# DIFF layers: the sub-norm's weights move from GpSimd's multiply into the copies of the turned blocks, and the first mixed block is turned one step sooner

## The chip, the cores and the metric
One core of one Trainium2 chip. The metric is the device time in microseconds (us) of one execution of the whole program. Every time in the profile is counted from the start of the span. PE is TensorE, DVE is VectorE, ACT is ScalarE, POOL is GpSimd, and SP is SyncE, which issues all the loads.

## The reference
Six transformer blocks run one after the other over 256 tokens of width 1024, all in float32. Blocks 0 and 1 have a hybrid mixer (HYB), block 1 with a mixture of eight experts. Blocks 2 to 5 are the second model's: differential attention (DIFF), MoBA, sliding window with sinks (SWA), and DIFF again, each followed by an MLP. What is changed lies in DIFF:

```python
p = jax.nn.softmax(s, axis=-1)
p = p[:, :, 0] - lam * p[:, :, 1]          # two maps of a head, combined
o = einsum('bhqk,bkhe->bqhe', p, v)        # 8 heads of width 128
o = rms_norm(o, sub_g) * (1.0 - lambda_init)
return o.reshape(B, S, H * DIFF_V_DIM) @ w_out
```

`sub_g` has 128 values, one per channel of a head, the same for all 8 heads. `rms_norm` divides each head's 128 channels of a token by their root mean square and multiplies by `sub_g`.

## The kernel before
Every product is made of three: both operands are split into a high part (ACT copies into the reduced type, `xt_hi`, `whi`) and a low part (DVE subtracts, `xt_lo`, `wlo`), and PE multiplies high by high, low by high and high by low. Weights come in units of 128 x 2048 (`load`), each split by ACT (L1691, L1695) and DVE (L2116, L2122) ahead of its use. Each engine's program is written out by hand; the engines meet only through semaphores, and within an engine everything stays in the written order.

In a DIFF layer (l = 2 and l = 5, n = 16 maps, two to a head) `soft_heads` of each engine runs over steps i. For a pair of maps j, j+1 (j even):

- PE turns the heads (`turn_heads`, L1468, at even i), makes the scores (`pair_scores`, L1593 and L1595, step j+1), turns the combined map (`turn_pair`, L1568, step j+5) and multiplies by the values (`pair_values`, L1580 to L1582, step j+6).
- DVE masks the scores and takes their maximum (L2551, step j+1), combines the two maps of a head (`combine`, L2471, step j+3), and in `finish_pair` (L2482 to L2491, step j+5) divides by the sum, takes the sum of squares of a head, asks for the ratio of the pair j+4 (`ask_ratio`, L2500, which waits for that pair's exponentials) and asks for the root.
- ACT copies the turned heads (L1806), takes the exponentials (L1821, L1823, map j at step j+2), and copies the turned map (L1839, step j+5).
- POOL runs `diff_norms`: per head the ratio of the pair two heads ahead (L711, L712), the root (L692), the block of y times the root (L729), and that block times `subg` (L730); then it raises `normed`.

The output projection needs y turned, in four mixed blocks of 128 x 512 (`turn_mixed`): PE transposes (L798) after enough heads are `normed` (4, 4, 6, 8 for blocks 0 to 3), ACT copies the high part (L1711), DVE takes the low part (L2140). Block 0 holds heads 0 to 3 of token tile 0, block 1 the same heads of tile 1, blocks 2 and 3 hold heads 4, 5 and 6, 7 of both tiles. `out_rows(l, n, t, parts)` multiplies unit n of `w_out` by the turned blocks of token tile t (L921); a part is one half of the unit, six matmuls of 512 columns. Block 0 is turned at step 15 = n-1, block 1 at step 18 = n+2; the two halves of `out_rows(l, 0, 0)` stand at steps 17 and 19. `out_project_diff` (L977) follows: rows of unit 1, block 2, half a unit for tile 1, block 3, and the rest.

`subg` is loaded once by broadcast to all partitions (L594), and the setup on DVE multiplies it by 1 - lambda_init (L2425). SP's loads of layer weights stand behind it in SP's queue.

Of the kernel before, what the change touches and what calls it, by code (L numbers as in the profile page):

```python
# [14 lines left out]
P = 128  # L15
# [157 lines left out]
def build(nc, A, out, bias_scratch):  # L173
    with ExitStack() as ctx:  # L174
        def sb(name, shape, dt=F32, scope=ctx):
            return scope.enter_context(nc.sbuf_tensor(name, shape, dt))
# [15 lines left out]
        sinks = sb("sinks", [P, 16])  # L192
        minus_sinks = sb("minus_sinks", [P, 16])
        lam = sb("lam", [P, 16])
        subg = sb("subg", [P, 2, 2 * HD])
        pos_i = sb("pos_i", [P, NT], I32)
        rope_f = sb("rope_f", [P, 6, NT, 8])
        rope_k = sb("rope_k", [P, NT, 8], I32)
# [222 lines left out]
        def mixed_cols(x_t, l, s):  # L421
            if s < 2 and KIND[l] != HYB:
                return x_t[:, 0:4, s * P:(s + 1) * P]
            n = mixed_block(l, s)
            return x_t[:, 2 * n:2 * n + 2, :].rearrange("p k (t s) -> p t k s", t=NT)
# [112 lines left out]
        def _(sp):  # L538
# [50 lines left out]
            def small():  # L589
                sp.dma_start(pos_i[:], A["positions_2"][0].rearrange("(t p) -> p t", p=P),  # L590
                             allow_slow_non_contiguous=True).then_inc(got["pos"], 16)
                for i, n in enumerate(("diff_lam_q1_2", "diff_lam_k1_2", "diff_lam_q2_2", "diff_lam_k2_2")):
                    sp.dma_start(lam_in[:, i], A[n].partition_broadcast(P)).then_inc(got["lam"], 16)
                sp.dma_start(subg[:], A["diff_subln_g_2"].partition_broadcast(P)).then_inc(got["subg"], 16)  # L594
                sp.dma_start(router_w[:], A["moe_router"][0].rearrange("(k p) e -> p k e", p=P)).then_inc(
                    got["router"], 16)
                sp.dma_start(sinks[:], A["swa_sinks_2"][0].partition_broadcast(P)).then_inc(got["sinks"], 16)
# [84 lines left out]
        @block.gpsimd  # L682
        def _(pool):
            pool.wait_ge(cst_loaded, 16)
            done = [0]

            def roots(n):
                for _ in range(n):
                    r = done[0]
                    w = ROOTS[r]  # L690
                    pool.wait_ge(var_ready, r + 1)
                    pool.tensor_tensor(rstd[:, r % 8, 0:w], var[:, r % 8, 0:w], cst[:, C_HALF:C_HALF + w],  # L692
                                       ALU.pow).then_inc(root_ready, 1)
                    done[0] += 1

            def stick_masks(l):
                for p in range(NSTICK[KIND[l]] // 2):
                    pool.wait_ge(z_read, HEAD0[l] + 2 * p + 2)
                    if p < 2:

                        pool.wait_ge(qk_turned, HEAD0[l] // 2 + 3)
                    else:
                        pool.wait_ge(pool_out, l + 1)
                    pool.tensor_tensor(stick_a(p), stick_z(p), stick_mask(C_STRICTNEG), ALU.add).then_inc(zm_ready, 1)

            def ratio(l, h):

                d = DIFF_SLOT[l]
                pool.wait_ge(var_ready, done[0] + 1)
                second = rinv[:, :, 2 * h + 1:2 * h + 2]  # L710
                link(pool.tensor_tensor(second, second, sums[:, :, 2 * h:2 * h + 1], ALU.mult))  # L711
                pool.tensor_tensor(second, second, lam[:, 10 + d:11 + d].rearrange("p c -> p c ()").broadcast_to([P, NT, 1]),  # L712
                                   ALU.mult).then_inc(root_ready, 1)
                done[0] += 1

            def diff_norms(l):

                ratio(l, 0)
                ratio(l, 1)
                for h in range(8):  # L720
                    if h + 2 < 8:
                        ratio(l, h + 2)
                    r = done[0]
                    roots(1)
                    pool.wait_ge(root_ready, r + 1)
                    v = y[:, :, h * P:(h + 1) * P]
                    scale = rstd[:, r % 8, 0:NT].rearrange("p t -> p t ()").broadcast_to([P, NT, P])
                    gains = subg[:, DIFF_SLOT[l]].rearrange("p c -> p () c").broadcast_to([P, NT, P])
                    link(pool.tensor_tensor(v, v, scale, ALU.mult))  # L729
                    ins = pool.tensor_tensor(v, v, gains, ALU.mult)  # L730
                    ins.then_inc(normed, 1)

            chain = [0]

            def link(ins):

                chain[0] += 1
                ins.then_inc(pchain, 1)
                pool.wait_ge(pchain, chain[0])

            for l in range(NL):
                if KIND[l] != HYB:
                    roots(2)
                if KIND[l] == SWA:
                    pool.wait_ge(rope_sin, 1)
                    pool.wait_ge(proj_ev, EV0[l + 1])
                    rotate(pool, link, [(8, 8)], late_tmp).then_inc(late_rope_done, 1)
                stick_masks(l)
                if KIND[l] == DIFF:
                    diff_norms(l)  # L750
                if l == 1:
                    roots(2)
                    pool.wait_ge(t_lo, 4 * 5)
                    for t in range(NT):
                        for half in range(2):
                            pool.memset(y[:, t, half * 512:(half + 1) * 512], 0.0).then_inc(added, 1)
                    roots(4)
                else:
                    roots(6 if KIND[l] == HYB else 2)
            roots(2)  # L760
# [3 lines left out]
        def _(pe):  # L764
# [21 lines left out]
            def turn_mixed(l, s):  # L786


                if KIND[l] in (MOBA, SWA):
                    pe.wait_ge(o_read, OG0[l] + (2, 2, 3, 4)[s])  # L790
                else:
                    pe.wait_ge(normed, NORMED0[l] + ((4, 4, 6, 6) if KIND[l] == HYB else (4, 4, 6, 8))[s])
                for i in range(4):
                    if s < 2 and KIND[l] != HYB:
                        t, k = s, i
                    else:
                        t, k = i // 2, 2 * mixed_block(l, s) + i % 2
                    mm = pe.transpose(bank[turned_at(l)[s]][:, i * P:(i + 1) * P], y[:, t, k * P:(k + 1) * P], ident)  # L798
                mm.then_inc(turned, 1)
# [672 lines left out]
            def soft_heads(l):  # L1472
# [3 lines left out]
                for i in range(n + (5 if kind == DIFF else 4)):  # L1476
# [38 lines left out]
                    if kind == DIFF:  # L1515
                        if i % 2 == 1 and 0 <= i - 5 < n:
                            turn_pair(l, i - 5)
                        if i == n - 2:
                            pe.wait_ge(proj_ev, EV0[l + 1])
                        if i % 2 == 0 and 0 <= i - 6 < n:  # L1520
                            pair_values(l, i - 6)
                        if i in (n - 1, n + 2):
                            turn_mixed(l, (i - n + 1) // 3)
                        if i == n + 1:
                            pe.wait_ge(t_lo, 4 * (3 * l + 1) + 1)
                            out_rows(l, 0, 0, (0,))
                        if i == n + 3:
                            out_rows(l, 0, 0, (1,))
                    j = i - 3
                    if 0 <= j < n and kind != DIFF:  # L1530
# [143 lines left out]
        def _(act):  # L1674
# [33 lines left out]

            def turn_mixed(l, s):
                act.wait_ge(turned, 4 * (3 * l + 1) + s + 1)  # L1710
                act.activation(mixed_cols(xt_hi, l, s), mixed_bank(l, s), ACT.Copy).then_inc(t_hi, 1)  # L1711

            def high_of_tokens(t):
                act.activation(xn_hi[:, t], x[:, t], ACT.Copy).then_inc(xn_hi_ready, 1)
# [93 lines left out]
            def soft_heads(l):  # L1808
                kind = KIND[l]
                n = NSOFT[kind]  # L1810
                for i in range(max(n + (4 if kind == DIFF else 3), late_parts(l) + 6)):
# [24 lines left out]
                    if 0 <= j < n and kind == DIFF and j % 2 == 0:  # L1836
                        s = SOFT0[l] + j
                        act.wait_ge(pt_done, s + 2)
                        act.activation(pt[:, s % 4], pt_bank(l, j)[:, 0:384], ACT.Copy).then_inc(pt_ready, 2)  # L1839
                    if kind == DIFF and i in (n - 1, n + 2):  # L1840
                        turn_mixed(l, (i - n + 1) // 3)
                    for u, half in late_used(l, i):
                        if kind == HYB or u != PLAN.proj[l][-1][-1]:
                            hi(u + NH, (half,))
# [254 lines left out]
        def _(dve):  # L2099
# [4 lines left out]
            def link(ins):  # L2104

                chain[0] += 1
                ins.then_inc(dchain, 1)
                dve.wait_ge(dchain, chain[0])
# [28 lines left out]

            def turn_mixed(l, s):
                dve.wait_ge(t_hi, 4 * (3 * l + 1) + s + 1)
                dve.tensor_tensor(mixed_cols(xt_lo, l, s), mixed_bank(l, s), mixed_cols(xt_hi, l, s).bitcast(F32),  # L2140
                                  ALU.subtract).then_inc(t_lo, 1)

            def ask_root(src, scale, eps, w):

# [245 lines left out]
            def setup():  # L2390
# [31 lines left out]
                    link(dve.tensor_scalar(lam[:, 10 + d:11 + d], lam[:, 8 + d:9 + d], -LAMBDA_INIT[l], None, ALU.add))  # L2422
                dve.wait_ge(got["subg"], 16)
                for l, d in DIFF_SLOT.items():
                    link(dve.tensor_scalar(subg[:, d], subg[:, d], 1.0 - LAMBDA_INIT[l], None, ALU.mult))  # L2425

            def add_bias(l, c, t):

# [100 lines left out]
            def soft_heads(l):  # L2529
# [8 lines left out]
                for i in range(n + 4):  # L2538
# [36 lines left out]
                    if i == n + 2 and kind == HYB:  # L2575
                        for s in range(2):
                            turn_mixed(l, s)
                    if i == n - 1 and kind == DIFF:
                        turn_mixed(l, 0)
                    j = i - 4  # L2580
                    if 0 <= j < n and kind != DIFF:
# [422 lines left out]
```

## Time and profile before

| | us |
|---|---|
| median of 3 runs | 2429.32 |
| lowest, highest | 2429.15, 2430.7 |
| the profiled execution | 2427.38 |
| its span, first to last instruction | 2425.6 |
| PE busy in the span | 2393.6 |
| DVE, ACT, POOL busy | 1725.7, 1450.1, 94.3 |

The span is the time between the first and the last instruction; the rest of an execution's time lies around it. Busy time of PE is modelled from pipelined matmuls, so a busy PE is not PE at its peak. A row of the timeline gives the start, the duration, the engine, the line, the operation, output and inputs, how many were merged, and in brackets the idle time before with who ended it. Starts of neighbouring rows are the better measure of pace, since ends of pipelined instructions overlap the next ones.

### The profile page before, as it was taken

The page shows a single profiled execution, that of the slowest core. Times are in us where ns is not written, and L with a number is a line of the kernel's source. Part 1 is how long each engine was busy: PE and PEld are TensorE (multiplying, and loading weights), DVE is VectorE, ACT ScalarE, POOL GpSimd, SP SyncE. Part 2 cuts the span into 40 slices and gives each one's busy share as a digit, 9 for nine tenths or more (in the row PEclk, how much of TensorE's full clock was granted, in tenths as well). Part 3 has the DMA queues.
Part 4 walks back from the last instruction along what each step waited for, and adds up shares of the span by engine and source line. Part 5 has one row for each costly group of instructions (what it writes and reads, how often), then busy time and mean ns, then how long its engine had stood idle before and what let it go on. Part 6 is the DMA issues. An engine that isn't in the chain of part 4 may idle for free. (4 is left out here: it accounts for less than half of the span.)

```text
span 2425.6 us, 31990 instructions
## 1 busy us (share of the span) xinstructions
PE 2393.6 (99%) x12546; PEld 2017.5 (83%) x12546; DVE 1725.7 (71%) x1911; ACT 1450.1 (60%) x1662; POOL 94.3 (4%) x130
## 2 busy tenths in 40 slices
PE   9999999999999999999999999999999999999998
PEld 7889978888888888888877788888888788887887
DVE  5565456888898998988995865666656665568565
ACT  6454354588888888888865554454444554456442
POOL 1000010000000000000000300000000000004000
PEclk9999999999999999999999999999999999999999
DMA  9266552699999999999965365452655265553553
GB/s 323 69 204 206 181 208 72 223 348 361 348 350 359 335 360 352 348 350 347 363 244 193 105 217 191 156 200 95 223 191 187 72 211 191 172 205 119 186 191 104
DMA packets 242366, 555.40 MB, mean 229 GB/s; under 512 B 10841, under 2 KB 36849, under 8 KB 241905
## 3 DMA queue, kind: packets, MB, share of 16 engines
q1 hardware_dynamic: 242160, 552.41, 65.5%
q8 instruction: 159, 2.61, 0.4%
q14 instruction: 47, 0.38, 0.0%
HBM read 551.31 MB, written 1.07 MB: 228 GB/s over the span
## 5 line engine op out<-in xcount | busy, mean ns | idle before, releaser
L2116 DVE TENSOR_TENSOR wlo<-raw,whi 128x2048 fp32r<-128x2048 f32 x486 | 1112.8, 2297 | 444.8 <-ACT whi L1691 444.0
L1691 ACT ACTIVATE whi<-raw 128x2048 fp32r<-128x2048 f32 x487 | 933.7, 1925 | 551.2 <-PE bank L921 141.6
L843 PE MATMUL bank<-whi,xt 128*128 128x512 f32 (+1 forms) x1056 | 311.3, 379 | 3.3 <-DVE xt L2133 1.3
L843 PEld LDWEIGHTS bank<-whi,xt 128*128 128x128 f32 x1056 | 189.5, 188 | 40.6 <-issue 3.1
L1234 PE MATMUL bank<-whi,xt 128*128 128x512 f32 (+1 forms) x768 | 222.0, 373 | 0.8 <-DVE e_hf L2744 0.8
L1077 PE MATMUL bank<-xt,whi 128*128 128x512 f32 x768 | 209.1, 394 | 0.0
L843 PE MATMUL bank<-wlo,xt 128*128 128x512 f32 (+1 forms) x528 | 197.6, 374 | 0.0
L921 PE MATMUL bank<-whi,h_hi 128*128 128x512 f32 x596 | 184.8, 391 | 0.0
L921 PE MATMUL bank<-whi,h_lo 128*128 128x512 f32 x596 | 183.9, 390 | 0.0
L921 PE MATMUL bank<-wlo,h_hi 128*128 128x512 f32 x596 | 183.9, 390 | 0.0
L1234 PEld LDWEIGHTS bank<-whi,xt 128*128 128x128 f32 x768 | 138.2, 189 | 24.8 <-DVE e_hf L2744 1.2
L1077 PEld LDWEIGHTS bank<-xt,whi 128*128 128x128 f32 x768 | 133.0, 189 | 19.1
L1234 PE MATMUL bank<-whi,odd_hi 128*128 128x512 f32 (+1 forms) x384 | 144.0, 375 | 0.1
L1234 PE MATMUL bank<-wlo,odd_hi 128*128 128x512 f32 (+1 forms) x384 | 142.9, 372 | 0.0
L1234 PE MATMUL bank<-wlo,xt 128*128 128x512 f32 (+1 forms) x384 | 142.8, 372 | 0.0
L1234 PE MATMUL bank<-whi,odd_lo 128*128 128x512 f32 (+1 forms) x384 | 142.7, 372 | 0.0
L921 PEld LDWEIGHTS bank<-whi,h_lo 128*128 128x128 f32 x596 | 111.9, 188 | 23.9
L921 PEld LDWEIGHTS bank<-wlo,h_hi 128*128 128x128 f32 x596 | 111.9, 188 | 23.7
L1081 PEld LDWEIGHTS bank<-xt,wlo 128*128 128x128 f32 x768 | 117.8, 189 | 16.2
L921 PEld LDWEIGHTS bank<-whi,h_hi 128*128 128x128 f32 x596 | 109.3, 188 | 20.6
L1081 PE MATMUL bank<-xt,wlo 128*128 128x256 f32 x768 | 122.1, 281 | 0.0
L692 POOL TENSOR_TENSOR rstd<-var,cst 128x1 f32<-128x1 f32 (+2 forms) x46 | 37.2, 808 | 2065.8 <-DVE var L2150 2051.1
(345 smaller groups left out, 3834.4 us busy)
## 6 DMA issues: line engine op xcount, KB each, us to landing
raw<-in_moe_wg SPq DMA_DIRECT2D x88, 1024.0 KB, 6.1
raw<-in_moe_wu SPq DMA_DIRECT2D x88, 1024.0 KB, 5.8
raw<-in_moe_wd SPq DMA_DIRECT2D x88, 1024.0 KB, 5.9
raw<-in_mlp_w_up SPq DMA_DIRECT2D x64, 1024.0 KB, 5.3
raw<-in_mlp_w_down SPq DMA_DIRECT2D x64, 1024.0 KB, 4.9
raw<-in_diff_w_in SPq DMA_DIRECT2D x24, 1024.0 KB, 5.2
raw<-in_w_in SPq DMA_DIRECT2D x19, 1024.0 KB, 7.8
raw<-in_moba_w_in SPq DMA_DIRECT2D x12, 1024.0 KB, 5.1
```

Source lines behind the costliest of these rows:

```text
L692: pool.tensor_tensor(rstd[:, r % 8, 0:w], var[:, r % 8, 0:w], cst[:, C_HALF:C_HALF + w], ALU.pow).then_inc(root_ready, 1)
L843: mm = pe.matmul(proj_bank(l, c, t)[:, 0:width], a[:, kx, t * P:(t + 1) * P], b[:, k, :], start=(kx == 0 and i == 0), stop=(kx == KT - 1 a ...
L921: mm = pe.matmul(bank[4 + 2 * t + half][:, :], a[:, k, t * P:(t + 1) * P], b[:, kk, half * 512:(half + 1) * 512], start=begin and i == 0, ...
L1077: pe.matmul(bank[f][:, :], hi[:, k, f * P:(f + 1) * P], xt[:, :, kx, :], start=kx == 0, stop=False, skip_group_check=True)
L1081: mm = pe.matmul(bank[f][:, 0:S], lo[:, k, f * P:(f + 1) * P], xt_hi[:, kx, :], start=False, stop=kx == KT - 1, skip_group_check=True)
L1234: mm = pe.matmul(bank[b][:, 0:width], a[:, kx, t * P:(t + 1) * P], w[:, k, :], start=(kx == 0 and i == 0), stop=(kx == KT - 1 and i == 2))
L1691: act.activation(whi[u % NH][:, :], raw[u % NR][:, :], ACT.Copy).then_inc(hi_ready[u % NR], 2)
L2116: dve.tensor_tensor(wlo[u % NR][:, :], raw[u % NR][:, :], whi[u % NH][:, :].bitcast(F32), ALU.subtract).then_inc(lo_ready[u % NR], 2)
```

## The change
POOL's second multiply per head is gone. `subg` is laid out the other way: channel d of a head stands in partition d, one column per DIFF layer, and since a turned mixed block has a head's channels on its partitions, the gain is a factor per partition there. ACT's copy takes it as its scale (with the function Identity instead of Copy), and DVE's low part becomes turned times gain minus high, in one instruction for blocks 0 and 1 and in two (one for each token tile) for blocks 2 and 3. The other layers keep their copies. Besides, block 0 is turned at step n-2 instead of n-1 on all three engines, and the two halves of the first output rows stand at steps n-1 and n+1 instead of n+1 and n+3.

```diff
-        subg = sb("subg", [P, 2, 2 * HD])
+        subg = sb("subg", [P, 32])
-                sp.dma_start(subg[:], A["diff_subln_g_2"].partition_broadcast(P)).then_inc(got["subg"], 16)
+                sp.dma_start(subg[:, 0:2], A["diff_subln_g_2"].rearrange("d p -> p d"),
+                             allow_slow_non_contiguous=True).then_inc(got["subg"], 16)
@@ POOL, diff_norms
-                    gains = subg[:, DIFF_SLOT[l]].rearrange("p c -> p () c").broadcast_to([P, NT, P])
-                    link(pool.tensor_tensor(v, v, scale, ALU.mult))
-                    ins = pool.tensor_tensor(v, v, gains, ALU.mult)
-                    ins.then_inc(normed, 1)
+                    pool.tensor_tensor(v, v, scale, ALU.mult).then_inc(normed, 1)
@@ PE, soft_heads
-                        if i in (n - 1, n + 2):
-                            turn_mixed(l, (i - n + 1) // 3)
-                        if i == n + 1:
+                        if i in (n - 2, n + 2):
+                            turn_mixed(l, (i - n + 2) // 4)
+                        if i == n - 1:
                             pe.wait_ge(t_lo, 4 * (3 * l + 1) + 1)
                             out_rows(l, 0, 0, (0,))
-                        if i == n + 3:
+                        if i == n + 1:
                             out_rows(l, 0, 0, (1,))
@@ ACT, turn_mixed and soft_heads
-                act.activation(mixed_cols(xt_hi, l, s), mixed_bank(l, s), ACT.Copy).then_inc(t_hi, 1)
+                gain = subg[:, DIFF_SLOT[l]:DIFF_SLOT[l] + 1] if KIND[l] == DIFF else 1.0
+                act.activation(mixed_cols(xt_hi, l, s), mixed_bank(l, s), ACT.Identity if KIND[l] == DIFF else ACT.Copy,
+                               scale=gain).then_inc(t_hi, 1)
-                    if kind == DIFF and i in (n - 1, n + 2):
-                        turn_mixed(l, (i - n + 1) // 3)
+                    if kind == DIFF and i in (n - 2, n + 2):
+                        turn_mixed(l, (i - n + 2) // 4)
@@ DVE, turn_mixed, setup and soft_heads
-                dve.tensor_tensor(mixed_cols(xt_lo, l, s), mixed_bank(l, s), mixed_cols(xt_hi, l, s).bitcast(F32),
-                                  ALU.subtract).then_inc(t_lo, 1)
+                if KIND[l] == DIFF:
+                    gain = subg[:, DIFF_SLOT[l]:DIFF_SLOT[l] + 1]
+                    parts = [(mixed_cols(xt_lo, l, s), mixed_bank(l, s), mixed_cols(xt_hi, l, s))]
+                    if s > 1:
+                        parts = [tuple(a[:, t] for a in parts[0]) for t in range(NT)]
+                    for low, src, high in parts:
+                        ins = dve.scalar_tensor_tensor(out=low, in0=src, scalar=gain, in1=high.bitcast(F32),
+                                                       op0=ALU.mult, op1=ALU.subtract)
+                    ins.then_inc(t_lo, 1)
-                    link(dve.tensor_scalar(subg[:, d], subg[:, d], 1.0 - LAMBDA_INIT[l], None, ALU.mult))
+                    link(dve.tensor_scalar(subg[:, d:d + 1], subg[:, d:d + 1], 1.0 - LAMBDA_INIT[l], None, ALU.mult))
-                    if i == n - 1 and kind == DIFF:
+                    if i == n - 2 and kind == DIFF:
                         turn_mixed(l, 0)
```

## Rows read from the trace of the kernel before

**Rows 1.** The page, part 1: busy time, share of the span, instructions.
```profile
PE 2393.6 (99%) x12546; PEld 2017.5 (83%) x12546; DVE 1725.7 (71%) x1911; ACT 1450.1 (60%) x1662; POOL 94.3 (4%) x130
```

**Rows 2.** PE's waits, whole span: us in total, times, longest us.
```profile
PE bank L1568 <- DVE z L2471: 3.0, 4, 1.2
...
PE bank L921 <- DVE wlo L2122: 0.5, 2, 0.2
```

**Rows 3.** Windows: stretch, length, busy us per engine, clock, DMA share, GB/s.
```profile
2193.00:2227.00 34.00, 31.37 (x190) 24.73 (x189) 29.17 (x104) 21.44 (x60) 20.76 (x34) 1.00 0.19 63
```

**Rows 4.** Timeline, layer 5, DVE and POOL: combinations with and without POOL beside them.
```profile
2193.41 1.74 DVE L2471 SCALAR_TENSOR_TENSOR z<-z,rinv 128x128 f32<-128x128 f32 x2
2193.44 0.61 POOL L729 TENSOR_TENSOR y<-y,rstd 128x256 f32<-128x256 f32 x1
2194.14 0.73 POOL L730 TENSOR_TENSOR y<-y,subg 128x256 f32<-128x256 f32 x1
...
2214.40 0.75 DVE L2471 SCALAR_TENSOR_TENSOR z<-z,rinv 128x128 f32<-128x128 f32 x2 [0.53 <-POOL rinv L712]
```

**Rows 5.** Timeline of PE, layer 5: scores and the next turned pair, twice.
```profile
2194.31 0.60 PE L1595 MATMUL bank<-qk 64*128 64x256 f32 x4
2195.20 0.55 PE L1568 MATMUL bank<-cst,z 128*128 128x128 f32 x3 [0.28 <-DVE z L2471]
...
2199.84 0.60 PE L1595 MATMUL bank<-qk 64*128 64x256 f32 x4
2200.37 0.55 PE L1568 MATMUL bank<-cst,z 128*128 128x128 f32 x3
```

**Rows 6.** Timeline of PE, end of layer 5, from the last heads' turn.
```profile
2205.96 0.60 PE L1468 MATMUL bank<-cst,h_qkv 128*128 128x128 f32 x4
...
2207.92 0.49 PE L1593 MATMUL bank<-qk 64*128 64x128 f32 x4 [0.20 <-DVE nmx L2551]
...
2212.18 0.55 PE L1568 MATMUL bank<-cst,z 128*128 128x128 f32 x3 [1.22 <-DVE z L2471]
2212.78 1.20 PE L921 MATMUL bank<-whi,xt 128*128 128x512 f32 x4
...
2214.27 0.38 PE L1580 MATMUL bank<-h_qkv,pt 128*128 128x128 f32 x2
...
2217.66 1.18 PE L921 MATMUL bank<-whi,xt 128*128 128x512 f32 x4
...
2222.89 0.66 PE L798 MATMUL bank<-cst,y 128*128 128x128 f32 x4 [0.37 <-POOL y L730]
```

**Rows 7.** Timeline of POOL, end of layer 5: the fourth head's multiply.
```profile
2207.89 0.62 POOL L729 TENSOR_TENSOR y<-y,rstd 128x256 f32<-128x256 f32 x1
```

**Rows 8.** Timeline of ACT, end of layer 5: exponential of map 13, first and last.
```profile
2208.14 0.38 ACT L1821 ACTIVATE z<-z,nmx 128x128 f32<-128x128 f32 x1
...
2208.93 0.19 ACT L1823 ACTIVATION_READ_ACCUMULATOR z<-z,nmx 128x1 f32 x1
```

**Rows 9.** Timeline of DVE, end of layer 5: ratio asked, block 0's low half.
```profile
2209.77 0.18 DVE L2500 RECIPROCAL rinv<-sums 128x4 f32<-128x4 f32 x1
...
2212.05 0.68 DVE L2140 TENSOR_TENSOR xt<-bank,xt 128x512 fp32r<-128x512 f32 x1
```

**Rows 10.** ACT's groups by line and shape: busy us, mean ns, idle before.
```profile
L1823 ACT ACTIVATE z<-z,nmx 128x256 f32<-128x256 f32 x76 | 37.7, 496 | 0.0
...
L1737 ACT ACTIVATE h_mix<-bank 128x256 f32<-128x256 f32 x8 | 3.0, 380 | 5.7 <-PE bank L843 5.7
```

**Rows 11.** DMA issues: size and median us from issue to landing.
```profile
subg<-in_diff_subln_g SPq DMA_DIRECT2D x1, 128.0 KB, 6.3
...
pos_i<-in_positions SPq DMA_DIRECT2D x1, 1.0 KB, 4.6
```

**Rows 12.** ACT by line: duration ns min/median/max, first and last start us.
```profile
L1821 ACT ACT_TABLE_LOAD  x1: 1283/1283/1283, 1317.4 to 1317.4; - x1
...
L1862 ACT ACTIVATE h_f<-bank x8: 598/602/609, 1390.9 to 2257.6; 128x512 f32<-128x512 f32 x8
```

More of the change, by code:

```diff
@@ L2139, in turn_mixed @@
                 dve.wait_ge(t_hi, 4 * (3 * l + 1) + s + 1)
-                dve.tensor_tensor(mixed_cols(xt_lo, l, s), mixed_bank(l, s), mixed_cols(xt_hi, l, s).bitcast(F32),
-                                  ALU.subtract).then_inc(t_lo, 1)
+                if KIND[l] == DIFF:
[7 more added lines that the diff above has]
+                    ins.then_inc(t_lo, 1)
+                else:
+                    dve.tensor_tensor(mixed_cols(xt_lo, l, s), mixed_bank(l, s),
+                                      mixed_cols(xt_hi, l, s).bitcast(F32), ALU.subtract).then_inc(t_lo, 1)
             def ask_root(src, scale, eps, w):
```

## The prediction

> **What bounds the kernel now.** I read the page's part 1 first: TensorE (PE) is busy for 2393.6 of 2425.6 us [rows 1], so only about 32 us of the span can be won by taking waits away, and whatever delays PE by a microsecond delays the end by one. The second view is the waits of PE over the whole span: the largest single entry is the turned pairs of probabilities (L1568) that wait for VectorE's (DVE's) combination of two maps (L2471), 3.0 us in 4 waits; the low half of a weight (L2122) costs 0.5 in 2 [rows 2]. Both belong to the ends of the two DIFF layers, l = 2 and l = 5, which is all that the diff touches after the setup. The window of the second of these ends, layer 5, shows PE busy 31.37 of 34 us at the full granted clock (1.00, the 2.4 GHz level), DVE 29.17, ACT 21.44 and POOL 20.76 [rows 3]. Layer 2's end is the same to the instruction, 859 us earlier; I work out layer 5 and count it twice. PE's idle time in the window is 34 - 31.37 = 2.6 us, so **5.3 us in both is the most that this change could win**.
>
> In what follows I cut 2200 off: 7.92 is 2207.92.
>
> **The gains multiply leaves POOL.** L730 goes: one of 0.73 us for each of 8 heads in a layer [rows 4], which gives a head's normed block 0.7 us sooner. POOL is not the bound, so what counts is who waits for it. First, DVE. A combination is two instructions that read two tiles each from SBUF. Alone the two take 0.75 us; where POOL's L729 and L730 run beside them they take 1.74 [rows 4]. The start times in that group show how: the first begins with L729 (0.61) and the second is held by L730. Without L730 one of the two stalls stays, 0.6 of L729, and the pair costs about 0.7 + 0.4 = 1.1 instead of 1.74: **0.6 us of DVE back** at each of the three early collisions of a layer. The page "SBUF — State Buffer" of the Trainium skill, section "Who interferes with whom", says that a DVE instruction with two SBUF inputs and a GpSimd instruction that reads SBUF exclude each other for a whole instruction, whichever starts first. By that rule the pair gets back the stall under L730 and no more, 0.6 and not the whole 1.0 by which it is slowed; the two start times in the rows agree.
>
> What PE gets of it before the end: the turned pair at 2195.20 starts 0.89 after L1595, where the next one starts 0.53 after it [rows 5], so 0.36 us of waiting for the combination goes and PE arrives at the last heads' turn (5.96 [rows 6]) 0.36 sooner, at 5.60. DVE gains 0.2 at first (it then waits for ACT's exponentials) and 0.75 by the third collision.
>
> **The end of the layer, step by step.** PE's order after the change is: turn of heads 14 and 15, values 8, *mixed block 0*, scores 14, turned pair 10, *output rows half 0*, values 10, turned pair 12, *output rows half 1*, values 12, mixed block 1, turned pair 14, values 14. No matmul is added or taken away; the question is only where PE stands.
> - Mixed block 0 needs the fourth head's norm. POOL's multiply for it starts at 7.89 now [rows 7] and ends 0.62 later; with DVE's 0.75 it ends at 7.75. PE, which starts scores 14 at 7.92 now behind a wait of 0.20 and a filling of its pipe [rows 6], is free at about 7.2, **waits 0.6** and turns the block at 7.80. Scores 14 then start at 7.80 + 0.4 = 8.20 instead of 7.92, and turned pair 10 at 9.05.
> - On ACT the copy of the block now stands ahead of the exponential of head 13. That one starts at 8.14 now and is done at 9.12 with its two halves and read-outs [rows 8]; behind the copy (8.5 to 9.15) it starts at 9.1 and is done at 10.1, **1.0 later**.
> - Who waits for that: DVE's finish of pair 8 asks for the ratio of heads 12 and 13, which needs that exponential. It asks at 9.77 now [rows 9] and will at 10.15. Only then comes the low half of block 0, 10.3 to 10.95; it starts at 12.05 now.
> - Output rows half 0 wait for that low half: 11.05. PE has nothing from 9.3 to 11.05: **a new wait of 1.7 us**, in the place of the one of 1.2 at 12.18, which goes. A half costs 14.27 - 12.78 = 1.49 [rows 6].
> - So values 10 at 12.5, turned pair 12 at 13.2 (its combination is done by 13.0: scores from 10.9, 1.1 of masks, 1.0 of combination), half 1 at 13.45, values 12 at 14.9, mixed block 1 at 15.6, turned pair 14 at 16.0. Between it and values 14 there is now no output row that covers the copy of the transposed probabilities (ACT has block 1 ahead of it): values 14 at 17.35, **1.1 us of wait**. Output rows of the second unit follow at 17.95; they start at 17.66 now [rows 6]. So this loop costs 0.65 against the 0.36 brought along: 0.3 late.
> - The last head: its sum of squares no longer meets L730 (now 0.5 lost) and POOL's own multiply is gone (0.7). Block 3 is turned at 22.89 now, behind a wait of 0.37 for POOL and a filling of PE's pipe [rows 6]; without it PE would be there near 22.35, so at 22.6 or 22.65 after the change, and the norm is there at about 22.0. **Block 3 at 22.6: 0.3 sooner.** Of this 0.1 is lost in the rows of the last unit, which wait for a weight's low half (0.2 per layer [rows 2]) that ACT starts after its copy of block 3.
>
> Sum: 0.2 us sooner per layer, **0.4 us in both**.
>
> **The copies that change.** ACT's copy of a turned block takes a factor per partition. No row has that form from PSUM; bounds: a plain copy of 128x256 takes 380 ns and an exponential of the same size with a column of biases 496 [rows 10], so between 0 and 0.12 more per copy. I take 0.1 as the exponential also reads a column; it is in the times above. The low half becomes a product and a difference in one DVE instruction. From below it is no dearer than now: it still reads one tile from PSUM and one from SBUF. Blocks 2 and 3 are two instructions instead of one: one start-up more, under 0.1 us, covered by the 2.9 us of output rows of unit 2 that PE has after block 3. The page "ScalarE: Activation LUTs", section "What ACT_TABLE_LOAD costs", puts such a pointer operand at about 93 ns; by it the sum would not change by 0.05.
>
> **The load of the gains** becomes 256 single elements instead of rows. The load of now lands after 6.3 us; the one vector that already comes element by element, the positions, after 4.6 [rows 11]. It is first read in the setup behind layer 0's first dense groups, after the whole of layer 0's output projection, so even ten times the landing is hidden. POOL's and SP's queues wait for nothing new. The scaling in the setup is two columns instead of two rows, 0.1 us of DVE less beside a weight that ACT has not copied yet: nothing.
>
> **Base.** The profiled execution took 2427.38 us outside for a span of 2425.6, and is 1.94 under the median 2429.32 of the runs; the difference of 0.4 is taken off the median: **2428.9 us**.
>
> **Rivals.**
> 1. *The loop bites harder* (to 2430.3, not beyond 2431.5). If DVE's 0.6 does not come back (POOL's remaining multiply falls so that it holds both instructions of a combination, which is free to happen since both engines shift), the fourth norm ends at 8.51, PE turns block 0 at 8.57, and everything behind is 0.8 later than above: 0.5 late per layer at block 3, +1.0. For it: POOL starts within 0.03 us of the combination in the collision shown [rows 4], by the semaphore that both follow, so their order is not chance and stays. Chance 0.17.
> 2. *The gain is larger* (2425.3 to 2427.8). If ACT or DVE reach the new order with less queueing than I have, the 1.7 and the 1.1 us waits shrink; half of each away is 1.4 per layer, 2.8 in both: 2426.1. Against it: the exponential of head 13 is plainly behind the copy in ACT's program. Chance 0.16. The idle time bounds it at 2424.0.
> 3. *A table load on ACT* (slower, about 2437). The copies of the DIFF layers change their function from Copy to Identity, which this kernel never used. The exponentials' set is loaded once at 1317.4 for 1283 ns [rows 12]. If Identity is not in that set, block 0 pays a load before it and one after it (exponentials 13 to 15 follow), and block 1 one more, all on the loop that PE waits for: 3 x 1.28 = 3.85 per layer, 7.7 in both. The point from which it decides: one load at block 0 alone, twice 2.56, is already beyond 0.2%. Against it: Relu (L1862) runs at 1390.9 with the exponentials' set and no load [rows 12]. Chance 0.03. By the same page's section on table sets the cheap functions, identity by name, stand in every set; then this rival is out.
>
> **Chances.** The forecast with a spread of about 0.8 either way has 0.62; the rivals 0.17, 0.16 and 0.03; 0.02 is for what I don't see. A measurement of this kernel can tell about 0.2%, 4.9 us, from no change. Faster by more would need nearly all the idle time: 0.02. Slower by more: the table load, 0.04. Within: 0.94. The range leaves out the table load and the far ends of rivals 1 and 2: 2426.8 to 2431.0; the runs of before alone spread over 1.5 us.
>
> **What would show it.** Right: combinations of about 1.1 us where 1.7 stood; a wait of about 0.6 of block 0's transposes (L798) for POOL's L729; the largest wait of the end, near 1.7, before the first output rows (L921) for DVE's low half; one near 1.1 before the last values (L1580); none before block 3; the stretch from the turn of the last heads to block 3 about 17.0 us as now (16.93). Wrong: ACT_TABLE_LOAD in these windows; combinations still at 1.7; the wait before the first output rows under 1 us.

## The result, and the profile after

| | before | after |
|---|---|---|
| median (us) | 2429.24 of 4 runs | 2448.00 of 4 runs |
| lowest, highest | 2427.96, 2430.70 | 2447.74, 2449.79 |
| span of the profiled execution | 2425.6 | 2448.0 |

After takes 1.008 times as long as before, with a 95% interval of 1.0067 to 1.0093: 18.8 us slower. The forecast was 2428.9, its range ended at 2431.0, and slower by over 0.2% had a chance of 0.04. The prediction was wrong.

The page of after, part 1, against [rows 1]:

```profile
PE 2414.0 (99%) x12546; PEld 2019.9 (83%) x12546; DVE 1721.3 (70%) x1915; ACT 1451.0 (59%) x1662; POOL 82.2 (3%) x114
```

PE has as many instructions as before (12546) and is busy for 20.4 us more. It is idle for 34.0 us, against 32.0. So the loss is no wait: TensorE's own work has grown longer. It did not grow in the windows that the prediction looked at, either. A stretch of 100 us in the middle of the experts, in a layer that the diff does not touch (windows: stretch, length, busy us per engine with instructions, clock, DMA share, GB/s), first before and then after:

```profile
600.00:700.00 100.00, 99.68 (x491) 84.08 (x490) 89.33 (x61) 84.05 (x81) 0.00 (x0) 1.00 0.99 350
```

```profile
600.00:700.00 100.00, 99.70 (x486) 83.21 (x485) 88.20 (x60) 83.31 (x78) 0.00 (x0) 1.00 0.98 346
```

PE is as busy and its clock is the same, but it gets 486 matmuls done instead of 491. PE's groups by line and shape (busy us, mean ns of one, idle before) show which matmuls these are. Before:

```profile
L843 PE MATMUL bank<-whi,xt 128*128 128x512 f32 x896 | 281.4, 395 | 2.5 <-DVE xt L2133 1.3 <-DVE wlo L2116 1.0 <-DVE wlo L2918 0.2
...
L921 PE MATMUL bank<-whi,h_hi 128*128 128x512 f32 x596 | 184.8, 391 | 0.0
L1234 PE MATMUL bank<-whi,odd_hi 128*128 128x512 f32 x320 | 125.8, 393 | 0.0
...
L1312 PE MATMUL bank<-whi,e_hi 128*128 128x512 f32 x352 | 109.4, 390 | 0.1
```

After (two lines up in the file):

```profile
L841 PE MATMUL bank<-whi,xt 128*128 128x512 f32 x896 | 281.3, 395 | 2.5 <-DVE wlo L2116 1.1 <-DVE xt L2133 1.1 <-DVE wlo L2928 0.3
...
L919 PE MATMUL bank<-whi,h_hi 128*128 128x512 f32 x596 | 187.7, 396 | 0.0
L1232 PE MATMUL bank<-whi,odd_hi 128*128 128x512 f32 x320 | 127.4, 398 | 0.0
...
L1310 PE MATMUL bank<-whi,e_hi 128*128 128x512 f32 x352 | 111.1, 395 | 0.1
```

In all of these the weight (`whi`) is the moving operand of 512 columns, and the second name is the stationary one, which PEld loads ahead of the matmul. With `xt` as the stationary operand a matmul of L841 costs what it did (the `xt` matmuls of L1232 are 2 ns dearer in this one execution, 394 for 392, but 392 again in e2_before_shifted below, which is just as slow). With `h_hi`, `e_hi` or `odd_hi` each one costs 5 ns more, and so do their siblings with the low halves. There are 3 x 596 + 3 x 352 + 3 x 320 = 3804 of them, and 3804 x 5 ns = **19.0 us**, which is the loss within 0.2 us.

### The profile page after: what moved, and what is told of

Same layout as the page of the kernel before. It is cut to its first block and busy times, and to the rows that moved or that the text cites. A ratio compares the mean times of both kernels' runs of the same rounds, so it can differ in the third digit from the quotient of the medians.

```text
span 2448.0 us, 31978 instructions
## 1 busy us (share of the span) xinstructions
PE 2414.0 (99%) x12546; PEld 2019.9 (83%) x12546; DVE 1721.3 (70%) x1915; ACT 1451.0 (59%) x1662; POOL 82.2 (3%) x114
## 5 line engine op out<-in xcount | busy, mean ns | idle before, releaser
L841 PE MATMUL bank<-whi,xt 128*128 128x512 f32 (+1 forms) x1056 | 311.2, 379 | 3.3 <-DVE wlo L2116 1.1
L1232 PE MATMUL bank<-whi,xt 128*128 128x512 f32 (+1 forms) x768 | 223.4, 375 | 0.8 <-DVE e_hf L2754 0.8
L841 PEld LDWEIGHTS bank<-whi,xt 128*128 128x128 f32 x1056 | 189.5, 188 | 40.4 <-issue 2.9
L841 PE MATMUL bank<-wlo,xt 128*128 128x512 f32 (+1 forms) x528 | 197.5, 374 | 0.0
L1232 PEld LDWEIGHTS bank<-whi,xt 128*128 128x128 f32 x768 | 138.8, 189 | 25.3 <-DVE e_hf L2754 1.2
L1232 PE MATMUL bank<-whi,odd_hi 128*128 128x512 f32 (+1 forms) x384 | 145.5, 379 | 0.1
L1232 PE MATMUL bank<-wlo,odd_hi 128*128 128x512 f32 (+1 forms) x384 | 144.3, 376 | 0.0
L1232 PE MATMUL bank<-whi,odd_lo 128*128 128x512 f32 (+1 forms) x384 | 144.2, 376 | 0.0
L1232 PE MATMUL bank<-wlo,xt 128*128 128x512 f32 (+1 forms) x384 | 143.6, 374 | 0.0
L841 PEld LDWEIGHTS bank<-wlo,xt 128*128 128x128 f32 x528 | 99.4, 188 | 18.2
```

The source lines that it names most:

```text
L841: mm = pe.matmul(proj_bank(l, c, t)[:, 0:width], a[:, kx, t * P:(t + 1) * P], b[:, k, :], start=(kx == 0 and i == 0), stop=(kx == KT - 1 a ...
L1232: mm = pe.matmul(bank[b][:, 0:width], a[:, kx, t * P:(t + 1) * P], w[:, k, :], start=(kx == 0 and i == 0), stop=(kx == KT - 1 and i == 2))
```

## What differs: the place of the tiles

`h_hi`, `e_hi` and `odd_hi` are in no line of the diff. But the diff makes `subg` smaller, from 256 to 32 floats per partition, that is from 1024 to 128 bytes. Tiles lie in SBUF one behind another in the order in which they are declared, so all that are declared behind `subg` start 896 bytes lower. In the compiled programs:

| tile | use | starts before | mod 256 | starts after | mod 256 |
|---|---|---|---|---|---|
| `raw`, `whi`, `wlo`, `xt` | ahead of `subg` | unchanged | 128 | unchanged | 128 |
| `h_hi`, `e_hi` (one place) | behind `subg` | 167040 | 128 | 166144 | 0 |
| `odd_hi` | behind `subg` | 209024 | 128 | 208128 | 0 |

My theory from here on was that the stationary operand's place against the moving operand's place, modulo some power of two, sets the pace. Its rivals were that the edits themselves cost the 19 us (the copies, the order), that the absolute place counts, and that any move of the tiles costs it.

## Experiments on the place

**Whose loss is it?** All of after's edits, with `subg` as large as before (only its first columns are used), so that every tile has its old place.

```
-        subg = sb("subg", [P, 32])
+        subg = sb("subg", [P, 256])
```

> The changed kernel, but subg keeps its old size of 256 floats a partition (the rest of it unused), so that every tile behind it stays where it was before. Layout theory: the 18.8 us come only from the tiles behind subg, which start 896 bytes lower in each partition (h_hi, e_hi, odd_hi and their low parts at 256 instead of 128 bytes past a multiple of 1024), where the 512-column matmuls that take them as stationary tile start every 232 ns instead of 227; then this kernel takes 2428 to 2430 us and the pace is 227 ns everywhere. Rival, the change's own work (new order, copies with a factor): it stays at 2448.

Measured: 2429.42 us (2428.08 to 2431.43, 11 runs) against 2428.49 of before (27 runs), ratio 1.0004 [0.9995, 1.0013]. The loss is gone, with every instruction of the diff in place. The other direction, before with one unused tile and nothing else:

```
         subg = sb("subg", [P, 2, 2 * HD])
+        pad = sb("pad", [P, 32])
```

> The kernel before with 32 unused floats a partition behind subg, so that the tiles behind it start 256 bytes past a multiple of 1024, as in the changed kernel, and nothing else is changed. Layout theory: about 2448 us, 232 ns a matmul for the stationary tiles h, e and odd, 227 for xt. Rival, the change's own work: 2429.

Measured: 2447.64 us (2 runs), ratio 1.0077 [1.0059, 1.0096]. 128 unused bytes per partition slow the untouched kernel by 19 us. Its group of PE, to be held against L921 of before:

```profile
L922 PE MATMUL bank<-whi,h_hi 128*128 128x512 f32 x596 | 187.7, 396 | 0.0
```

**Absolute or relative?** The same unused tile ahead of all the others, so that moving and stationary tiles shift together.

```
+        pad = sb("pad", [P, 32])
         with ExitStack() as loads:
             raw = ...
```

> The kernel before with 32 unused floats ahead of all its tiles: every tile, moving and stationary, starts 256 bytes past a multiple of 1024. If what counts is where the stationary tile lies against the moving one (whi, wlo): 2429 us, as nothing moves against anything. If what counts is where the stationary tile itself starts: slower than 2448, about 2459, since the matmuls with xt as stationary tile (some 2400 with 512 columns) slow down too by 5 ns each.

Measured: 2428.5 us (8 runs), ratio 0.9996 [0.9986, 1.0006]. Here `h_hi` starts at 0 modulo 256 as in after, and nothing is lost: the place of one tile against the other counts, not that of either alone.

**Which modulus?** After again, with other sizes of `subg`. The distance of the stationary tiles from their place of before, modulo 512 bytes, is 0 for 128 floats, 32 bytes for 136, 64 for 144, 256 for 64 and 384 for 96 (128 in after itself).

```
-        subg = sb("subg", [P, 32])
+        subg = sb("subg", [P, 128])     # then 136, 144, 64, 96
```

> The changed kernel with subg of 128 floats: the tiles behind it start 640 bytes past a multiple of 1024, that is 128 past a multiple of 512, like the moving tiles. If the stretch that counts is 512 bytes or less: 2429 us. If it is 1024 or more: not 2429, nearer to 2448.

> The changed kernel with the tiles behind subg moved so that they lie 32 bytes from the moving tiles modulo 512 (160 past a multiple of 512). If any offset costs the same (the row of 512 bytes of a stationary tile then crosses a line that the moving tiles' rows keep to): 232 ns a matmul, 2448 us. If the cost grows with the offset (5 ns at 128 bytes): 228 ns, 2434 us. If only multiples of 128 are bad: 227 ns, 2429 us.

> The same at 64 bytes from the moving tiles modulo 512. Any offset the same: 232 ns, 2448 us. Growing: 229 to 230 ns, 2438 us. Only multiples of 128: 227 ns, 2429 us.

> The same at 256 bytes modulo 512. If the stretch that counts is 512 bytes (or 512 divided by an odd share): slower, 232 ns and 2448 us if any offset costs the same, up to 237 ns and 2466 us if the cost grows. If the stretch is 256 bytes: 227 ns, 2429 us.

> The changed kernel with subg of 96 floats: h, e and odd lie 384 bytes from the moving tiles modulo 512, that is 128 modulo 256. What the runs so far say is a stretch of 256 bytes: slow, 232 ns, about 2448 us, the same as the changed kernel. If instead 256 and 384 were both good places (a stretch of 512 with a good half): 2429 us.

| kernel | distance modulo 512 (and 256) | us | ratio [95%] | start to start with `h`, `e` or `odd` stationary, median ns |
|---|---|---|---|---|
| e1_old_place | 0 (0) | 2429.42 | 1.0004 [0.9995, 1.0013] | 227 |
| e4_half_place | 0 (0) | 2429.65 | 1.0003 [0.9993, 1.0013] | 227 |
| e7_rel256 | 256 (0) | 2429.94 | 1.0005 [0.9994, 1.0016] | 227 |
| after | 128 (128) | 2448.00 | 1.0080 [1.0067, 1.0093] | 232 |
| e8_rel384 | 384 (128) | 2449.83 | 1.0087 [1.0069, 1.0106] | 232 |
| e5_rel32 | 32 (32) | 2449.10 | 1.0087 [1.0057, 1.0116] | 233 |
| e6_rel64 | 64 (64) | 2450.34 | 1.0092 [1.0063, 1.0121] | 233 |

The column of medians comes from the starts of the single matmuls with 512 columns that follow one another, with the high and the low parts of the three tiles. I had held 512 bytes for the modulus; e7_rel256 disproves that and e8_rel384 agrees: the tested distances cost nothing at multiples of 256 bytes and some 20 us at 32, 64, 128 and 384. The loss does not grow with the distance: the four ratios lie between 1.0080 and 1.0092, and their intervals overlap. That any move of the tiles costs it is out too: in e4_half_place they start 512 bytes lower than in before and in e7_rel256 768. The group of e7_rel256:

```profile
L919 PE MATMUL bank<-whi,h_hi 128*128 128x512 f32 x596 | 184.8, 391 | 0.0
```

The pace itself can be seen in PE's timeline in the experts, where each row merges two matmuls and the rows start 0.45 us apart (e1_old_place, first) or 0.46 to 0.48 (after, second):

```profile
858.08 0.62 PE L1310 MATMUL bank<-whi,e_hi 128*128 128x512 f32 x2
858.53 0.61 PE L1310 MATMUL bank<-whi,e_lo 128*128 128x512 f32 x2
858.98 0.62 PE L1310 MATMUL bank<-wlo,e_hi 128*128 128x512 f32 x2
859.43 0.62 PE L1310 MATMUL bank<-whi,e_hi 128*128 128x512 f32 x2
```

```profile
866.20 0.64 PE L1310 MATMUL bank<-whi,e_hi 128*128 128x512 f32 x2
866.68 0.62 PE L1310 MATMUL bank<-whi,e_lo 128*128 128x512 f32 x2
867.14 0.62 PE L1310 MATMUL bank<-wlo,e_hi 128*128 128x512 f32 x2
867.60 0.64 PE L1310 MATMUL bank<-whi,e_hi 128*128 128x512 f32 x2
```

**Another tile.** If it is the relation and not these tiles, then `xt` can be made the slow one in its turn: before, with `xt` moved by 128 bytes and the tiles behind `subg` by 128 + 384 = 512.

```
+        pad = sb("pad", [P, 32])
         xt = sb("xt", [P, 2, KT, S], F32R)
...
         subg = sb("subg", [P, 2, 2 * HD])
+        pad2 = sb("pad2", [P, 96])
```

> The kernel before with 32 unused floats ahead of xt and 96 behind subg: whi and wlo stay, xt, x, y and the constants lie 128 bytes on, and the tiles behind subg are 512 bytes on, so that h, e and odd lie as before against whi and wlo modulo 512. Layout theory: now the 512-column matmuls with xt as stationary tile, some 3300 (1344, 564, 960 and 480 of the four lines), take 232 ns and those with h, e and odd 227: 2429 + 16 = about 2445 us. Rival, that the large tiles of the expert and dense stages alone are touchy: 2429.

Measured: 2441.09 us (3 runs), ratio 1.0052 [1.0029, 1.0075]: 12.8 us slower, where about 16 were expected. The groups have changed sides:

```profile
L845 PE MATMUL bank<-whi,xt 128*128 128x512 f32 x896 | 285.3, 399 | 2.5 <-DVE xt L2135 1.3 <-DVE wlo L2118 0.8 <-DVE wlo L2920 0.4
...
L1236 PE MATMUL bank<-whi,xt 128*128 128x512 f32 x640 | 201.9, 397 | 0.7 <-DVE e_hf L2746 0.5 <-issue 0.2
L923 PE MATMUL bank<-whi,h_hi 128*128 128x512 f32 x596 | 184.7, 391 | 0.0
```

`xt` costs 4 to 5 ns more per matmul, `h_hi` nothing, so the relation holds for this tile as well; the size was put too high. Added up from start to start against before, the 2240 matmuls with `whi` and `xt` lose 4.5 ns each, but the 1120 with `wlo` and `xt` only 2.3: together 12.6 us. Why these lose less I can't read from the traces.

The matmuls of 256 columns do not lose: with `xt` stationary their median start to start is 120 ns in before and 119 here. And one group of 512 columns hardly changes, the one in which the roles are turned round, with `xt` moving and the weight stationary. Before, and e9_xt_shifted:

```profile
L1077 PE MATMUL bank<-xt,whi 128*128 128x512 f32 x768 | 209.1, 394 | 0.0
```

```profile
L1079 PE MATMUL bank<-xt,whi 128*128 128x512 f32 x768 | 210.3, 395 | 0.0
```

Its starts lie 234 ns apart (median) in before, at the same place modulo 256, and 233 in e9_xt_shifted, 128 bytes off; in the sum it costs 1.2 us, where 5 ns each would be 3.8. So the 227 and 232 ns belong to matmuls whose moving tile is the weight.

## Experiments on the edits themselves

With the tiles at their old places the diff does what it says, and its two halves can be parted. The table gives PE's start of each step in layer 5, counted from the turn of the last heads.

| step of PE | before | forecast | e1_old_place | e10 gains | e11 order | e12 |
|---|---|---|---|---|---|---|
| mixed block 0 | 3.47 | 2.20 | 2.30 | 2.97 | 3.47 | 2.30 |
| first output rows | 6.82 | 5.45 | 5.59 | 6.51 | 6.60 | 4.52 |
| output rows, half 1 | 9.66 | 7.85 | 7.99 | 9.36 | 11.11 | 6.93 |
| last values (14) | 11.12 | 11.75 | 11.88 | 10.84 | 15.30 | 10.81 |
| mixed block 3 | 16.93 | 17.0 | 17.25 | 16.11 | 21.23 | 16.15 |

**The gains alone**: after's copies and POOL program, the old order of the steps, `subg` at 256 floats.

```
-                        if i in (n - 2, n + 2):
-                            turn_mixed(l, (i - n + 2) // 4)
-                        if i == n - 1:
+                        if i in (n - 1, n + 2):
+                            turn_mixed(l, (i - n + 1) // 3)
+                        if i == n + 1:
...
-        subg = sb("subg", [P, 32])
+        subg = sb("subg", [P, 256])
```

> The changed kernel with subg in its old size and with the old order (block 0 turned at step n-1, the output rows' halves at n+1 and n+3): only the gains move. Theory: DVE's combinations at about 1.1 instead of 1.7 us and the norms 0.7 sooner, and nothing given back to a new loop: the stretch from the turn of the last heads to block 3 falls from 16.9 to about 16.3 us, 0.36 comes before it, so about 2 us less in both layers, 2426.5 against 2428.4. Rival, that these waits just move to the next one: within 0.3 us of before.

Measured: 2426.2 us (2424.38 to 2428.33, 11 runs) against 2428.86 of before (23 runs), ratio 0.9988 [0.9979, 0.9997]. Block 3 is turned 0.82 us sooner after the last heads in each layer, and the last heads 0.36 sooner, which makes 2.4 us in both. The kernel is 2.7 us faster than before, as expected (2426.5), with an interval of 0.7 to 5.1. PE's waits (us in total, times, longest), against the 3.0 in 4 waits for L2471 in [rows 2]:

```profile
PE bank L1566 <- DVE z L2481: 2.3, 2, 1.2
```

**The order alone**: before, with only the new steps for block 0 and the two halves.

```
-                        if i in (n - 1, n + 2):
-                            turn_mixed(l, (i - n + 1) // 3)
-                        if i == n + 1:
+                        if i in (n - 2, n + 2):
+                            turn_mixed(l, (i - n + 2) // 4)
+                        if i == n - 1:
...
-                        if i == n + 3:
+                        if i == n + 1:
...
```

> The kernel before with only the new order; POOL still multiplies by the gains. Theory: block 0 waits 1.1 us for the fourth norm, and the first output rows about 1.8 for its low half, as head 13's exponential stands behind ACT's copy; the stretch from the last heads to block 3 grows from 16.9 to about 17.5 us, so 2429.5 against 2428.4. Rival, that the new order fills the wait for the combination as it seems meant to: the stretch falls by about 1 us.

Measured: 2435.75 us (2433.43 to 2438.05, 7 runs), ratio 1.003 [1.0019, 1.0041]: 6.9 us slower than before, where I had expected under 1, and a stretch to block 3 of 17.5 us where it is 21.23 in layer 5 and 19.78 in layer 2. Two things are in it. PE's timeline at the end of layer 5:

```profile
2212.69 0.66 PE L798 MATMUL bank<-cst,y 128*128 128x128 f32 x4 [1.71 <-POOL y L730]
...
2215.83 2.08 PE L921 MATMUL bank<-whi,xt 128*128 128x512 f32 x4 [0.97 <-DVE xt L2140]
2217.70 1.05 PE L921 MATMUL bank<-wlo,xt 128*128 128x512 f32 x2
2218.55 0.63 PE L1580 MATMUL bank<-h_qkv,pt 128*128 128x128 f32 x2
```

First, block 0 waits for POOL's second multiply, which is still there: 1.71 us before L798, and the block at 3.47 instead of 2.30. Second, the first output rows take 2.72 us (2215.83 to 2218.55), where in e1_old_place they take 1.49. The windows say why (columns as above; the first busy time is PE's, and the figure behind the five busy times is the granted clock):

```profile
2208.00:2210.00 2.00, 1.82 (x16) 1.21 (x15) 1.92 (x9) 1.47 (x7) 0.54 (x2) 1.00 0.74 164
2210.00:2212.00 2.00, 0.91 (x6) 0.74 (x6) 2.00 (x11) 1.45 (x5) 1.76 (x5) 1.00 0.95 353
2212.00:2214.00 2.00, 1.31 (x12) 0.94 (x12) 0.96 (x6) 0.62 (x2) 0.64 (x1) 1.00 0.02 7
2214.00:2216.00 2.00, 1.03 (x6) 0.50 (x5) 1.05 (x6) 1.34 (x5) 0.71 (x3) 0.59 0.00 0
2216.00:2218.00 2.00, 2.00 (x5) 1.62 (x6) 2.00 (x8) 1.64 (x7) 1.67 (x3) 0.50 0.00 0
2218.00:2220.00 2.00, 2.00 (x9) 1.81 (x9) 0.11 (x1) 0.22 (x2) 0.00 (x0) 0.50 0.00 0
```

The granted clock falls to 0.50, the 1.2 GHz level, from 2214.4 to 2221.2 (read from windows of half a microsecond), after three stretches in which PE was busy for 0.91, 1.31 and 1.03 of 2 us. In layer 2 it is low from 1350.8 to 1354.2. In layer 5, PE needs 6.37 us from the first output rows to values 12 (6.60 to 12.97), against 3.87 in e1_old_place (5.59 to 9.46): 2.5 us for the clock. In layer 2, block 0 to the first output rows takes 3.96 us against 3.13 in layer 5 of the same kernel, where the clock was still full there: 0.8. So 3.3 of the 7.6 us between the two spans (2433.2 and 2425.6) are put down to the clock. Of the other 4.3, which I put down to the order, 3.8 stand in the two stretches from the last heads to block 3; the rest was not traced. One of the seven executions had a mean clock of 1.000; it took 2433.43, 4.6 over before, which agrees. What divides this kernel from e1_old_place I can't read from the runs: there PE is busy for 1.46, 1.25 and 1.45 us in the three stretches from 2208 to 2214, and the clock stays at 1.00.

**The copy out of the exponential's way**: after with the old places, and ACT's copy of block 0 one step later in ACT's program, behind the exponential of head 13.

```
+                    if kind == DIFF and i == n - 1:
+                        turn_mixed(l, 0)
                     j = i - 5
                     if 0 <= j < n and kind == DIFF and j % 2 == 0:
...
-                    if kind == DIFF and i in (n - 2, n + 2):
-                        turn_mixed(l, (i - n + 2) // 4)
+                    if kind == DIFF and i == n + 2:
+                        turn_mixed(l, 1)
```

> The changed kernel with subg in its old size, and with ACT's copy of block 0 placed behind the exponential of head 13 instead of ahead of it. Theory of the loop: the exponential is done 1 us sooner, the ratio of heads 12 and 13 with it, and the wait ahead of the first output rows falls from 1.7 to about 1.1 us; the stretch from the last heads to block 3 falls from 17.25 to about 16.7 us. If the loop is not what PE waits for, the stretch stays at 17.25.

Measured: 2426.1 us (2424.95 to 2427.88, 11 runs), ratio 0.9988 [0.9979, 0.9997]. The wait before the first output rows shrinks from 1.30 us to 0.23, more than I had expected:

```profile
2211.74 1.20 PE L919 MATMUL bank<-whi,xt 128*128 128x512 f32 x4 [0.23 <-DVE xt L2148]
```

and block 3 comes 1.1 us sooner than in e1_old_place (16.15 against 17.25). So the new order's price was the exponential of head 13 behind the copy; without it the order costs nothing against e10_gains_only (2426.2), and gains nothing.

## Why the prediction was wrong

**The step that failed.** Under "The load of the gains" the prediction went through the new layout of `subg`: its DMA, its landing, its scaling, all at nothing. The new size of the tile was not priced at all, in the sum or among the bounds, though the diff shows it in its first line. It was worth 19 us (e1_old_place, e2_before_shifted). No rival had it either: beyond rival 1's 2431.5 only the table load's 0.03 and the 0.02 "for what I don't see" stood on the slow side. All of the prediction's attention went to 5.3 us of waits, while 3804 matmuls, each 5 ns longer, outweighed them. "PE is busy 99%" had been read as "only waits can move"; the other way to read it is that any change of the matmuls' own pace goes straight into the time.

**The rest of the sum** can be read in e1_old_place, which has everything of the diff but the move of the tiles. It took 2429.42, inside the stated range, and against its own before +0.9 (within what can be told from no change); the forecast was -0.4. That it comes so near to the forecast is in part luck, as the last point below shows.

- *DVE's combination* was put at 1.1 us without L730. It takes 1.18 to 1.19 at the three early collisions of each layer, where [rows 4] have 1.74 (timeline of e1_old_place):

```profile
2194.79 1.19 DVE L2481 SCALAR_TENSOR_TENSOR z<-z,rinv 128x128 f32<-128x128 f32 x2
```

  At the fourth it takes 1.10, as it did before. The 0.36 us that PE was to bring along to the last heads came: the turns of the heads lie 5.17 us apart where one pair lay 5.53 apart before. That one stall goes and no more is what the section "Who interferes with whom" of the Trainium skill's page "SBUF — State Buffer" led to; the trace agrees.
- *Block 0 waits for the norm*: forecast 0.6, measured 0.54. *The largest wait is before the first output rows*: forecast 1.7, measured 1.30 in layer 5 and 1.65 in layer 2. The two waits for the copy of the transposed probabilities are 0.8 and not 1.1. PE's waits in after:

```profile
PE bank L919 <- DVE xt L2146: 3.0, 2, 1.7
...
PE bank L1578 <- ACT pt L1839: 1.6, 2, 0.8
...
PE bank L796 <- POOL y L729: 1.1, 2, 0.5
```

- *The chain behind it* was right in its order: copy, exponential of head 13, ratio, low half, output rows. Timeline of e1_old_place, ACT and DVE:

```profile
2209.95 0.69 ACT L1710 ACTIVATE xt<-bank,subg 128x512 fp32r<-128x512 f32 x1 [0.89 <-PE bank L796]
2210.54 0.39 ACT L1821 ACTIVATE z<-z,nmx 128x128 f32<-128x128 f32 x1
...
2211.61 0.18 DVE L2510 RECIPROCAL rinv<-sums 128x4 f32<-128x4 f32 x1 [1.24 <-ACT z L1823]
...
2211.75 0.74 DVE L2146 SCALAR_TENSOR_TENSOR xt<-bank,subg,xt 128x512 fp32r<-128x512 f32 x1
```

  All milestones in the table above lie within 0.25 us of the forecast, each a little late: the fourth norm by 0.09; the low half, put at no dearer than the plain subtraction, takes 0.74 where I reckoned with 0.65; and 0.1 is the pipe's filling behind the last values, which I had not counted.
- *The copy with a factor* takes 0.69 us where one without takes 0.60, so 0.09 more; 0.1 was taken. The Trainium skill's page "ScalarE: Activation LUTs", section "What ACT_TABLE_LOAD costs", gives about 93 ns for such an operand; the trace agrees.
- *Blocks 2 and 3 in two instructions* cost 0.88 us each on DVE (0.68 in one before [rows 9]): 0.2 more, where I gave under 0.1. PE's waits list none for them.
- *Rival 3*, a table load for Identity, did not happen: after has as many ACT_TABLE_LOAD as before. *Rivals 1 and 2*: the first did not occur (combinations at 1.10 to 1.19), the second neither in the diff as it stands; e10_gains_only and e12_copy_behind_exp reach the time it named, 2426.2 and 2426.1, because in them the copy stands behind the exponential.
- *Block 3* came at 17.25 and not 17.0 in layer 5. Less the 0.36 brought along that is nothing, where 0.2 us sooner were forecast. In layer 2 it came at 17.61 (16.96 before), which is 0.26 later after the 0.39 brought along there. The prediction counted layer 5 twice, since the two ends are alike in before; in e1_old_place they are not. In layer 2 DVE asks for the ratio of heads 12 and 13 only 0.45 us after the exponential's end, in layer 5 0.10 after it, and the rows' wait is longer by just this 0.35. What holds DVE there the trace does not show. So the order of the waits was right, and the net was 0.2 too good in layer 5 and 0.5 in layer 2. The other 1.2 of the 1.4 us between the two profiled spans (2427.0 and 2425.6) lie outside these stretches and were not traced; two executions of one kernel differ by as much.

What stays open: why the pace depends on the two places modulo 256 bytes, and what distances other than those tested cost. The stationary tiles were always moved against `raw`, `wlo` and `whi` together, so that it is the moving tile's place that they must share, and not that of `raw`, which the loads fill, is my reading and was not tested apart. Whether the order alone would keep the full clock under another arrangement was not tried.

## What to carry to other kernels

When a diff changes the size of an on-chip tile, list which tiles lie behind it and where each then starts, before any wait is looked at; padding the tile to its old size is a test of one line and here also the repair. If a kernel's TensorE is busy 99% of the time, count its matmuls and ask what could change the pace of each: 5 ns on 3804 of them outweighed all the waits in play. Of two edits that a change brings together, time each alone: here the gains were worth 2.7 us, and the new order, as the diff has it, gave them back.

## What the runs showed of the hardware

- A matmul of 512 columns whose moving tile is a weight (`whi`, `wlo`) starts 227 ns after the one before it when its stationary tile starts at the same place modulo 256 bytes as the weight (distances of 0 and 256, also both tiles moved together), and 232 to 233 ns after it at distances of 32, 64, 128 and 384. In the groups of `h_hi` that is 391 against 396 ns.
- With `xt` moving and the weight stationary the starts lie 234 ns apart at a distance of 0 and 233 at 128 (before, e9_xt_shifted).
- Matmuls of 256 columns showed no such loss: with `xt` stationary 120 ns in before and 119 in e9_xt_shifted, with `odd` stationary 120 in before, 119 in after and 114 at a distance of 64 (e6_rel64).
- A combination of two instructions on DVE takes 0.74 us alone, 1.10 to 1.19 beside one GpSimd multiply of 0.6 us and 1.74 beside two (e1_old_place, before).
- A kernel that differs from another by the order of a few steps can lose TensorE's full clock where the other keeps it: in e11_order_only it was at its 1.2 GHz level for 6.8 and 3.4 us in the two layers, at a cost of about 3.3 us.
